# A fused decoder layer on one core: every streamed tile moved to a multiple of 512 bytes in SBUF

## The reference, cut to what matters

```
xn = rmsnorm(x, mix_norm_g)                    # x: 512 tokens x 1024
p  = xn @ w_in                                 # 4 mixers' inputs and 4 x 1024 gates
ya, yb, yc, yd = mlstm(...), short_conv(...), mamba2(...), stick_breaking(...)   # 512 wide each
lifted = y_i @ w_lift[i]                       # 512 -> 1024, for each branch i
x  = x + (sum_i sigmoid(gate_i) * lifted_i) @ w_out
h  = causal_dwconv(rmsnorm(x, ffn_norm_g) @ w_up) + conv_b     # 1024 -> 2 x 2816
x  = x + (silu(h[:, :2816]) * h[:, 2816:]) @ w_down            # 2816 -> 1024
return rmsnorm(x, final_norm_g)
```

## Time and profile before

| | |
|---|---|
| time, median of 3 runs | 1050.11 us (1050.05 to 1050.98) |
| profiled execution, first to last instruction (its span) | 1048.9 us |
| TensorE matmuls | busy 1031.9 us (98%), 4724 instructions |
| weight loads | busy 837.0 us (80%) |
| VectorE, ScalarE, GpSimd | busy 593.3 us (57%), 424.8 us (41%), 67.7 us (6%) |
| mean granted TensorE clock | 0.995 of 2.4 GHz |

### The profile page before, as it was taken

How to read it: one execution, slowest core, us unless ns; L and a number is a source line. 1 busy time by engine, 2 the same in 40 slices (tenths; PEclk the granted TensorE clock), 3 DMA queues, 4 the chain that set the end, 5 groups by cost and what they waited for, 6 DMA issues and landing times.

```text
span 1048.9 us, 12635 instructions
## 1 busy us (share of the span) xinstructions
PE 1031.9 (98%) x4724; PEld 837.0 (80%) x4724; DVE 593.3 (57%) x764; ACT 424.8 (41%) x515; POOL 67.7 (6%) x74
## 2 busy tenths in 40 slices
PE   8999999999999999999999999989999999999996
PEld 6797888887777887777888888868888888888886
DVE  6834753766676576554454365687566566533323
ACT  5514446554435333434342334454444433423222
POOL 5610000000000000000000000400000000000002
PEclk9999999999999999999999999999999999999999
DMA  6331232223321333342242222413332232243312
GB/s 243 112 105 69 81 87 77 81 90 104 98 90 63 124 131 131 108 148 81 98 165 98 101 81 101 170 64 108 100 100 82 97 100 80 67 168 95 95 56 80
DMA packets 32024, 108.24 MB, mean 103 GB/s; under 512 B 3684, under 2 KB 5860, under 8 KB 31600
## 3 DMA queue, kind: packets, MB, share of 16 engines
q1 hardware_dynamic: 29520, 93.86, 27.1%
q0 software_dynamic: 2320, 13.69, 3.8%
q10 hardware_dynamic: 144, 0.14, 0.1%
HBM read 103.42 MB, written 4.25 MB: 103 GB/s over the span
## 4 chain that ended last, share of the span: by engine, by line
PE 93%; DVE 4%; ACT 2%; issue 1%; DMA 1%; DVEq 0%; SPq 0%; ACTq 0%
PE gb L411 81%; PE gb L444 4%; DVE w_lo L983 1%; PE xb L594 1%; PE gb L522 1%; PE xb L554 1%; PE xb L547 1%; PE xb L534 1%; PE xb L411 1%; ACT w_hi L699 1%; PE xb L511 1%; DMA raw<-w_stream 1%; DVE y_lo L991 1%; PE gb L462 1%; PE xb L582 0%
## 5 line engine op out<-in xcount | busy, mean ns | idle before, releaser
L983 DVE TENSOR_TENSOR w_lo<-raw,w_hi 128x1024 fp32r<-128x1024 f32 (+2 forms) x181 | 218.1, 1206 | 353.6 <-ACT w_hi L699 353.0
L699 ACT ACTIVATE w_hi<-raw 128x1024 fp32r<-128x1024 f32 (+2 forms) x181 | 183.8, 1017 | 424.9 <-PE gb L411 390.9
L411 PE MATMUL gb<-xn_hi,w_hi 128*128 128x512 f32 x720 | 285.7, 397 | 0.0
L411 PE MATMUL gb<-xn_lo,w_hi 128*128 128x512 f32 x720 | 282.1, 392 | 0.0
L411 PE MATMUL gb<-xn_hi,w_lo 128*128 128x512 f32 x720 | 280.7, 390 | 0.0
L411 PE MATMUL gb<-y_hi,w_hi 128*128 128x512 f32 x400 | 160.8, 402 | 5.4 <-DVE y_lo L991 3.7
L411 PEld LDWEIGHTS gb<-xn_hi,w_hi 128*128 128x128 f32 x720 | 135.6, 188 | 31.3 <-issue 1.0
L411 PE MATMUL gb<-y_hi,w_lo 128*128 128x512 f32 x400 | 159.9, 400 | 0.0
L411 PEld LDWEIGHTS gb<-xn_lo,w_hi 128*128 128x128 f32 x720 | 135.6, 188 | 29.7 <-issue 1.4
L411 PE MATMUL gb<-y_lo,w_hi 128*128 128x512 f32 x400 | 159.0, 398 | 0.0
L411 PEld LDWEIGHTS gb<-xn_hi,w_lo 128*128 128x128 f32 x720 | 135.5, 188 | 29.4
(11 more groups left out here) (231 smaller groups left out, 1018.4 us busy)
## 6 DMA issues: line engine op xcount, KB each, us to landing
raw<-w_stream SPq DMA_DIRECT2D x149, 512.0 KB, 3.3
raw<-w_down SPq DMA_DIRECT2D x16, 384.0 KB, 3.0
abc<-scr_a POOLq DMA_DIRECT2D x8, 640.0 KB, 4.2
raw<-w_down SPq DMA_DIRECT2D x16, 320.0 KB, 2.8
x_in<-xT SPq DMA_DIRECT2D x8, 256.0 KB, 6.2
x<-xT POOLq DMA_DIRECT2D x1, 2048.0 KB, 8.7
scr_x<-x POOLq DMA_DIRECT2D x1, 2048.0 KB, 7.4
x<-scr_x POOLq DMA_DIRECT2D x1, 2048.0 KB, 8.5
```

What stands on the lines that cost most here:

```text
L411: ins = pe.matmul(out, w[:, r, lo:hi], rhs(k)[x], start=(first and n == 0 and q == 0), stop=(last_ and n == len(ks) - 1 and q == 2))
L699: act.activation(w_hi[:, r, 0:n], raw[:, r, 0:n], ACT.Copy).then_inc(S["hi_ready"], 1)
L983: dve.tensor_tensor(w_lo[:, r, 0:n], raw[:, r, 0:n], w_hi[:, r, 0:n].bitcast(F32), ALU.subtract)\
```

## The change

The map's base moves from 16512 to 16896, which is 33 times 512. After the constants the map is rounded up to the next multiple of 512 from its base. So every tile named above starts at a multiple of 512: the ring, the split weights and `xn` move up by 384 bytes, everything from `y_hi0` on by 800 bytes. The blocks of the small unit are padded from 96 to 128 columns in memory, so that they lie 512 bytes apart; the matmuls on them still use 96 columns. The unit's transfer has the same size as before, since a whole slot was always sent. No instruction is added, removed or moved, no wait is changed.

```
+LINE = 512
...
-    base = 16512
+    base = 16896
...
-    END_CONST = m.at
+    m.at = base + (m.at - base + LINE - 1) // LINE * LINE
     y_hi0 = m.put("y_hi0", [P, 4, T], F32R)
...
-                        ins = pe.matmul(gb(o)[0:96, :], w[:, u % RING, 96 * k:96 * k + 96], xn(k)[x],
+                        ins = pe.matmul(gb(o)[0:96, :], w[:, u % RING, P * k:P * k + 96], xn(k)[x],
...
-    small = np.zeros((D, 96), np.float32)
+    small = np.zeros((D, P), np.float32)
...
-    stream[U_SMALL, :, 0:KD * 96] = slabs(small)
+    stream[U_SMALL] = slabs(small)
```

## The result

The changed kernel takes 1037.27 us (median of 4 runs, 1036.68 to 1038.53) against 1050.55 us (4 runs, 1050.05 to 1051.21) for the kernel before on the same chip: a ratio of 0.9874, 95% interval 0.986 to 0.9888. Forecast: 1036.6. The profiled execution took 1038.53 us and spans 1036.8 us, 12.1 us less than before.

The account below looks back on a forecast made before the run. TensorE's matmul stream was taken to bound the kernel; 10.8 us from `y` and `h`, 2.6 from switching and 0.1 from the small unit make 13.5 off 1050.1, giving 1036.6 us, with a range from 1030 to 1044.5.

Parts of the forecast that it names:

- What bounds: Whole kernel: TensorE's matmuls, busy 98% of the span, set the time; shorter steps between them come out at the end.
- `y` and `h` take `xn`'s rate: 512-column matmuls on `y` and `h`: each step falls by 6.5 ns to 226.8 ns, 10.8 us off.
- `xn` and the weights unchanged: 512-column matmuls on `xn`: moving these tiles and the weights from offset 128 to 0 changes nothing.
- Rival 2: All 512-column steps: 128 is itself a bad start, 0 spares a second 6.5 ns each; about 1012 us, chance 6%.
- Rival 4: Each 512-column step: both TensorE streams starting on the same 512-byte line hinder each other; about 1058 us, chance 6%.
- Rival 3: `y` and `h` steps: rate belongs to tile's place, other readers or slice order, not its start; 1050 us, chance 7%.
- The switching surplus: 8 output and 44 up units: 0.05 us each for switching between `y` and `xn` disappears, 2.6 us off.
- The small unit: Its 24 matmuls with 96-column weight blocks go from 232.5 to 226.8 ns, 0.14 us off.
- From the span to the time: The runs' median, 1.2 us above the profiled span of 1048.9 us, keeps that excess after the change.
- The random term: Low granted clock after TensorE's gap around 688 us: falling otherwise or staying out moves the end by up to 2 us.

Follow-up runs that it names:

- e2: Changed kernel with its base at 16608, so all streamed tiles and weights start 224 bytes past a multiple of 512; 1037.44 us.
- e4: Changed kernel with padding of 64, 192 and 128 bytes putting `y` at 64 and 384 and `h` at 256 past a multiple of 512; 1044.24 us.
- e3: Kernel before with only the base moved to 16896, no rounding after the constants, small unit at steps of 384 bytes; 1050.6 us.
- e10: Kernel before with 160 bytes of padding after the constants, putting `y` and `h` 256 bytes from the weights' offset; 1037.98 us.
- e9: Changed kernel using only 64 of 128 columns of each weight block in the up loop and 32 in the down loop; 1043.59 us.
- e7: Changed kernel padded so `xn` starts at 480, `y` at 416 and 64, `h` at 448 past a multiple of 512, weights at 0; 1057.76 us.
- e8: Changed kernel on a base of 16640, padded so every low tile starts 128 bytes past a multiple of 256 and every high tile at one; 1051.1 us.
- e11: Changed kernel with split weights of 256-column units shifted in their ring slots, by 192 bytes for eight units and 64 for the last four down units; 1035.93 us.
- e1: Kernel before with only the rounding after the constants, so every streamed tile starts 128 bytes past a multiple of 512; 1037.91 us.

## Why the prediction was right

*What bounds.* TensorE's stream, with everything else hidden: right. Only its steps moved, and the saving came out at the end.

*`y` and `h` take `xn`'s rate* (10.8 of 13.5 us): right, 226.7 to 227.1 ns, and 32 up units make 768 x 226.6 ns = 174.0 us where 174.2 was forecast. The reason was half right. The prediction gave two readings of the start, not the weights' offset and not a multiple of 64, and could not part them; e2 and e4 show that only the first counts, and with a period of 256 bytes. The rule of the Trainium skill ("SBUF — State Buffer", the note on cachelines under the port swizzle) on lines of 16 bytes, by which nothing should change, doesn't describe it: all offsets here are multiples of 16, and steps of 226.7 and 233.3 ns stand beside each other.

*`xn` and the weights unchanged*: right, by e3 as well. Rival 2 is out, and so is its premise that 128 is itself a bad start. Rival 4, two streams hindering each other when they start alike, is out for 512 columns; for 256 it is true in small, 119.9 ns at a distance of 0 against 116.7 at 32. Rival 3, the tile's place, is out by e3 and e10: `y` moved by 384 bytes with the weights keeps its 233.3 ns, and moved by 160 bytes alone it takes 227.1.

*The switching surplus* (2.6 us): right. The stretch of 669 fell by 154.21 - 151.69 = 2.52 us, where its 273 matmuls on `y` at 6.5 ns give 1.8 and its surplus of 0.7 the rest. The prediction's reading of what is in that stretch was wrong, though. The timeline of before has nine half-and-half units there and seven lift units, not 12.5 and 5. Whole groups of a lift unit and two gate units start at 530.26 and 546.80: 16.54 us, where 24 x 233.3 + 48 x 226.8 ns make 16.49. So such a lift group carries 0.05 us of surplus too, and for the 16 of them up to 0.8 us were left out of the sum.

*The small unit* (0.14 us): mis-sized, 5.58 to 5.54 us, 0.04. The term took 128-column blocks' 226.8 ns for it; with 96 columns the step is 5.54 / 24 = 230.8 even at a common offset, and e9 shows the like for 64 and 32.

*From the span to the time* (1.2 us): too small. Every run on record with both numbers has its time 1.7 to 2.0 us above its span, 1038.53 against 1036.8 for the profiled one. The 1.2 set the median of other executions against the span of one. With 1.7 the same sum gives 1037.1, and the measured median is 1037.27.

*The random term* of up to 2 us was needed: about 1.3 us of the forecast gain of 13.5 went to the clock after the gap, and 12.1 show in the profiled span. The executions with the clock of before span 1035.0 and 1035.1 us, 13.9 and 13.8 less and within 0.4 of the forecast. That the time came within 0.7 us is in part luck: the lift groups left out make it shorter, the clock after the gap and the 0.5 us missing between span and time make it longer.

## What to carry to other kernels

In a kernel bound by a stream of matmuls, read the step from start to start by tile family, not the mean duration: 3% hid in a difference of 6.6 ns. For 512-column fp32r streams with 128-column weight blocks, place moving and stationary tiles at the same offset within 256 bytes; no absolute alignment was needed, and 160 bytes of padding did it. Another block width or column count has to be measured by itself, since the best distance for 256 columns was another.

## What the runs showed of the hardware that was not expected

- The step of a 512-column fp32r matmul depends on the distance between its two operands in SBUF, 226.7 to 234.3 ns, with a period of 256 bytes, and not on where either lies; one lift unit in e7 broke the pattern, 233.3 ns at a distance of 64 where 228.9 was usual. The Trainium skill ("TensorE: Matmul & The Clock Gate", "Step-by-step: what each phase is for") says that loading the next weights doesn't take read bandwidth from the running matmul. The trace doesn't bear that out here: with 226.7 and 233.3 ns on record and nothing but the distance changed, the two reads must affect each other somewhere; where was not found. Banks that repeat every 256 bytes would fit, and this is argued, not shown.
- Fewer columns in the weight block made the step longer: 226.7 ns at 128, 230.0 at 64, 231.7 at 32, at a distance of 0. That the stream locks into repeating patterns of steps (224 to 236 ns in e8) and can lock at two rates at one distance (e11, and the odd unit of e7) says that timing between the reads matters, not just their number. What the remaining 13 ns above 512 columns at 2.4 GHz are stays open.
- The granted clock fell at the end of TensorE's gap of about 4 us before the up loop, or just after it, and how long TensorE then worked at the low clock differed. Before, it started again at 692.23 us and had 0.60 to 696 and 0.97 to 700; in the changed kernel it started at 687.18 and had 0.50 from 688 to 692 and 0.84 to 696. From 10 to 14 us the clock was low in the profile of the changed kernel and at 1.00 in that of e1. Equal runs of the changed kernel span 1035.0 to 1036.8 us at mean clocks of 0.995 to 0.992, and a gain of a few tenths of a percent has to be read against that.
